# Grouped projection with keys and values first, roots kept per column, and rotation by copied halves

## The reference

```
def apply_rope(x, cos, sin):            # differential and grouped queries and keys
    x0, x1 = even and odd columns of a head
    out = stack([x0 * cos - x1 * sin, x0 * sin + x1 * cos])

q, k = rms_norm(q, gain), rms_norm(k, gain)   # per head of 64 columns
q, k = apply_rope(q), apply_rope(k)           # tokens only, not the context
attend(q, k, v)
```

## Time and profile before

| | |
|---|---|
| median of three runs | 2760.64 us |
| the profiled execution | 2751.36 us, span 2749.5 us |
| TensorE busy | 2554.8 us (93%) |
| VectorE busy | 1546.8 us (56%) |
| ScalarE busy | 901.0 us (33%) |
| GpSimd busy | 835.8 us (30%) |
| mean granted clock of TensorE | 0.955 of 2.4 GHz |
| chain that ended last | TensorE 77%, VectorE 12%, issue 5% of the span |

### The profile page before, as it was taken

One profiled execution on the slowest core, in us unless ns is written; L12 is line 12 of the kernel. 1 busy time (PEld: TensorE's weight loads), 2 busy tenths in 40 slices (PEclk: granted clock), 3 DMA queues, 4 the chain that ended last, 5 costly groups with the idle time before them and its releaser, 6 DMA issues.

```text
span 2749.5 us, 37446 instructions
## 1 busy us (share of the span) xinstructions
PE 2554.8 (93%) x14518; PEld 2085.7 (76%) x14518; DVE 1546.8 (56%) x2130; ACT 901.0 (33%) x1358; POOL 835.8 (30%) x445
## 2 busy tenths in 40 slices
PE   7899898999999988988989999999987997999998
PEld 5667886788877766866778888888775765788887
DVE  2366756667586765586455745645855475533232
ACT  3465123222233244345332122122224421433232
POOL 3333022554441221223222323222212320344443
PEclk9999998999998989999999999999987998999999
DMA  4212012545450100130023423322211020233222
GB/s 164 77 60 72 2 39 100 169 165 171 145 172 28 46 24 15 54 79 1 31 85 100 146 92 99 118 97 99 100 39 44 24 85 1 84 107 100 99 94 83
DMA packets 78422, 227.50 MB, mean 83 GB/s; under 512 B 21440, under 2 KB 23488, under 8 KB 77770
## 3 DMA queue, kind: packets, MB, share of 16 engines
q1 hardware_dynamic: 64056, 172.99, 19.2%
q10 hardware_dynamic: 14226, 52.54, 5.7%
HBM read 223.38 MB, written 2.12 MB: 82 GB/s over the span
## 4 chain that ended last, share of the span: by engine, by line
PE 77%; DVE 12%; issue 5%; ACT 2%; POOL 2%; DMA 0%; DVEq 0%; ACTq 0%; POOLq 0%
PE ps L270 19%; PE ps L271 19%; PE ps L272 19%; PE ps L732 3%; PE ps L747 3%; DVE rstd L641 2%; PE ps L763 2%; POOL w_lo L2183 2%; PE ps L410 1%; PE ps L341 1%; PE ps L343 1%; PE ps L342 1%; DVE ada_place L1004 1%; PE ps L2014 1%; PE ps L759 1%
## 5 line engine op out<-in xcount | busy, mean ns | idle before, releaser
L2183 POOL TENSOR_TENSOR w_lo<-ring,w_hi 128x1024 fp32r<-128x1024 f32 x293 | 714.4, 2438 | 1490.2 <-ACT w_hi L263 978.0
L270 PE MATMUL ps<-act_hi,w_hi 128*128 128x512 f32 x2264 | 841.6, 372 | 32.1 <-DVE mix_lo L915 10.9
L272 PE MATMUL ps<-act_hi,w_lo 128*128 128x512 f32 x2264 | 825.7, 365 | 0.0
L270 PEld LDWEIGHTS ps<-act_hi,w_hi 128*128 128x128 f32 x2264 | 428.3, 189 | 120.3 <-issue 21.0
L271 PE MATMUL ps<-act_lo_ffn,w_hi 128*128 128x512 f32 (+1 forms) x1408 | 514.4, 365 | 0.0
L272 PEld LDWEIGHTS ps<-act_hi,w_lo 128*128 128x128 f32 x2264 | 427.1, 189 | 72.3
L263 ACT CAST w_hi<-ring 128x1024 fp32r<-128x1024 f32 (+1 forms) x167 | 174.1, 1043 | 789.7 <-PE ps L272 671.8
L1004 DVE SCALAR_TENSOR_TENSOR ada_place<-ada_place 128x1024 f32<-128x1024 f32 x192 | 328.7, 1712 | 30.1 <-ACT ada_place L994 14.7
L271 PEld LDWEIGHTS ps<-act_lo_ffn,w_hi 128*128 128x128 f32 x1408 | 266.4, 189 | 42.2 <-issue 0.7
L1074 ACT CAST w_hi<-ring 128x1024 fp32r<-128x1024 f32 (+1 forms) x132 | 137.6, 1043 | 459.7 <-PE ps L272 459.7
L270 PE MATMUL ps<-hidden_hi,w_hi 128*128 128x512 f32 x704 | 256.7, 365 | 2.8 <-DVE hidden_lo L1140 1.6
(11 more groups left out here) (341 smaller groups left out, 3400.8 us busy)
## 6 DMA issues: line engine op xcount, KB each, us to landing
ring<-in_w_ffn SPq DMA_DIRECT2D x204, 512.0 KB, 3.3
ada_place<-in_w_ada ACTq DMA_DIRECT2D x96, 512.0 KB, 3.3
ring<-in_w_gdn SPq DMA_DIRECT2D x16, 512.0 KB, 3.3
ring<-in_w_hy SPq DMA_DIRECT2D x12, 512.0 KB, 3.3
ring<-in_w_dil_qk SPq DMA_DIRECT2D x8, 512.0 KB, 6.7
ring<-in_w_out SPq DMA_DIRECT2D x8, 512.0 KB, 3.3
ring<-in_w_diff_qk SPq DMA_DIRECT2D x8, 512.0 KB, 4.1
ring<-in_w_na_qk SPq DMA_DIRECT2D x8, 512.0 KB, 3.3
```

Source lines behind the costliest of these rows:

```text
L270: pe.matmul(out, w[0], x[0], start=start, stop=False)
L272: return pe.matmul(out, w[1], x[0], start=False, stop=stop)
L2183: pool.tensor_tensor(k.w_lo[:, a % SPLITS, :], k.ring[:, a % SLOTS, :], k.w_hi[:, a % SPLITS, :].bitcast(F32), ALU.subtract).then_inc(k.lo ...
```

## The change

There are three parts.

Rotation by halves. The columns of each head of the differential and grouped queries and keys are put in another order on the host: even ones in the first half of the head, odd ones in the second. The partner of a row is then 32 partitions away. ScalarE copies the tile from PSUM a second time, in four pieces of 32 partitions, each to the place of its partner (`swap_halves`), into one of two buffers in `mix`. VectorE multiplies the tile by gain and cosine, the swapped tile by the partner's gain and the signed sine, and adds (`rope_vector`). The rotation no longer needs the root, and the tile is multiplied by the reciprocal afterwards. The product with `rope_swap` goes.

Grouped projection. The order of units becomes keys, values, four of queries. Keys and values are the two units of `first_units`. Values are made like keys, copied to SBUF and turned by six transposes. For the queries the sums of squares are laid out with the tokens on the partitions and 8 columns (4 blocks x 2 heads), so root and reciprocal have 8 columns, not 512; eight products with the identity spread them again over the tile (`spread_roots`).

Feed-forward nets. ScalarE copies the upper halves of units 2 and 3 ahead of `ada_begin`.

```diff
-    ("w_gqa_qk", 5), ("w_gqa_v", 1), ("w_hy", 12), ("w_out_o", 8), ("w_ffn3", FFN_UNITS),
+    ("w_gqa", 6), ("w_hy", 12), ("w_out_o", 8), ("w_ffn3", FFN_UNITS),
...
+def swap_halves(s, dst, src):
+    for a in range(0, P, HD):
+        for to, at in ((a, a + HD // 2), (a + HD // 2, a)):
+            s.eng.copy(dst[to:to + HD // 2], src[at:at + HD // 2])
+def swapped(k, i):
+    return k.mix_flat[:, S * (i % 2):S * (i % 2 + 1)]
+def rope_vector(k, v, x, xs, gain, gain_swap):
+    link(v, v.eng.scalar_tensor_tensor(x, x, gain, k.const("cos", 0, S), ALU.mult, ALU.mult))
+    link(v, v.eng.scalar_tensor_tensor(xs, xs, gain_swap, k.const("sin", 0, S), ALU.mult, ALU.mult))
+    link(v, v.eng.tensor_tensor(x, x, xs, ALU.add))
...
-                else:
-                    pe.wait_ge(self.normed, self.b + j + 1)
-                    if j >= 1:
-                        pe.wait_ge(self.rotated, self.r + j)
-                    pe.matmul(k.bank(bank), k.const("rope_swap"), x[:, 0:S], start=True, stop=True).then_inc(self.swapped, 1)
...
             if i < n:
+                if self.jobs[i][5] is not None:
+                    if i >= 2:
+                        s.eng.wait_ge(self.normed, self.b + i - 1)
+                    swap_halves(s, swapped(k, i), src[:, 0:S])
                 s.eng.copy(back(x), blocks(src)).then_inc(self.evac, 1)
...
-                if what == "norm":
-                    v.eng.wait_ge(self.rooted, self.b + j + 1)
-                    if j < n:
-                        v.eng.wait_ge(self.evac, j + 1)
-                    link(v, v.eng.reciprocal(k.rstd[:, 0:size], k.probs[:, j % 2, 0:size]))
-                    v.eng.scalar_tensor_tensor(x, x, gain, k.rstd[:, 0:size], ALU.mult, ALU.mult).then_inc(self.normed, 1)
-                    v.eng.wait_ge(self.normed, self.b + j + 1)
+                if gain_swap is not None:
+                    v.eng.wait_ge(self.evac, self.e + j + 1)
+                    rope_vector(k, v, x[:, 0:S], swapped(k, j), gain, gain_swap)
+                v.eng.wait_ge(self.rooted, self.b + j + 1)
+                if j < n:
+                    v.eng.wait_ge(self.evac, self.e + j + 1)
+                link(v, v.eng.reciprocal(k.rstd[:, 0:size], k.probs[:, j % 2, 0:size]))
+                if gain_swap is None:
+                    ins = v.eng.scalar_tensor_tensor(x, x, gain, k.rstd[:, 0:size], ALU.mult, ALU.mult)
                 else:
-                    v.eng.wait_ge(self.swapped, self.r + j + 1)
-                    link(v, v.eng.tensor_tensor(k.probs_t[:, 0:S], k.bank(bank), k.const("sin", 0, S), ALU.mult))
-                    link(v, v.eng.tensor_tensor(x[:, 0:S], x[:, 0:S], k.const("cos", 0, S), ALU.mult))
-                    v.eng.tensor_tensor(x[:, 0:S], x[:, 0:S], k.probs_t[:, 0:S], ALU.add).then_inc(self.rotated, 1)
-                    v.eng.wait_ge(self.rotated, self.r + j + 1)
+                    v.eng.tensor_tensor(x[:, 0:S], x[:, 0:S], k.rstd[:, 0:S], ALU.mult)
+                    ins = v.eng.scalar_tensor_tensor(x[:, S:size], x[:, S:size], gain, k.rstd[:, S:size], ALU.mult, ALU.mult)
+                ins.then_inc(self.normed, 1)
+                v.eng.wait_ge(self.normed, self.b + j + 1)
...
-                upper(it, 2 * a, static and c == 0 and a == 0)
+                begun = static and c == 0 and a == 0
+                if not begun:
+                    upper(it, 2 * a)
...
-                upper(it, 2 * a + 1)
+                if not begun:
+                    upper(it, 2 * a + 1)
...
         if c == 0:
+            upper(0, 0, True)
+            upper(0, 1)
             f.ada_begin(s)
...
+def gqa_bank(t):
+    return 4 if t % 2 == 0 else 0
+def gqa_project_tensor(k, pe):
+    v0, evac = FIRST["w_gqa"], k.sem("gqa_evac")
+    squares, summed, rooted, normed = k.sem("head_squares"), k.sem("head_summed"), k.sem("head_rooted"), k.sem("head_normed")
+    first_units(k, pe, "w_gqa", k.h_hi, k.lo2, (S, CTX), (k.sem("norm_lo"), DT * LOWERED.index("mod_a1")))
+    def add(t):
+        job = GQA + 1 + t
+        pe.wait_ge(squares, job + 1)
+        pe.wait_ge(rooted, job)
+        for b in range(PAIRS):
+            last = pe.matmul(k.bank(6, 2, 2 * b), k.sq[:, (t + 1) % 2, b * P:(b + 1) * P], k.const("heads64")[:, 0:P:HD],
+                             start=True, stop=True)
+        last.then_inc(summed, 1)
+    def spread_roots(t):
+        pe.wait_ge(k.sem("gqa_inverted"), t + 1)
+        if t >= 1:
+            pe.wait_ge(normed, GQA + 1 + t)
+        for b in range(PAIRS):
+            for h in range(2):
+                at, r = 32 + 8 * (t % 2) + 2 * b + h, slice(HD * h, HD * h + HD)
+                last = pe.matmul(k.ps[r, 7 * 512 + b * P:7 * 512 + (b + 1) * P], k.small[:, at:at + 1].broadcast_to([P, HD]),
+                                 k.const("ident"), start=True, stop=True)
+        last.then_inc(k.sem("gqa_spread"), 1)
+    for t in range(4):
+        u = v0 + SPLITS + t
+        if t >= 1:
+            pe.wait_ge(evac, (1, 3, 4)[t - 1])
+        if u not in HALVED:
+            pe.wait_ge(k.lo_done, u + 1)
+        unit_products(k, pe, gqa_bank(t) // 2, u, k.h_hi, k.lo2, DT, (S,))
+        if t == 0:
+            pe.wait_ge(squares, GQA + 1)
+            pe.matmul(k.bank(6), k.const("heads64"), k.sq[:, 0, 0:S], start=True, stop=True)
+            pe.matmul(k.bank(7, CTX), k.const("heads64"), k.sq[:, 0, S:T], start=True, stop=True).then_inc(summed, 1)
+            pe.wait_ge(evac, 2)
+            for b in range(6):
+                last = pe.transpose(k.bank(5, P, b * P) if b < 4 else k.bank(1, P, (b - 4) * P),
+                                    k.probs[:, 1, b * P:(b + 1) * P], k.const("ident"))
+            last.then_inc(k.sem("gqa_turned"), 1)
+        else:
+            add(t - 1)
+        if t >= 2:
+            spread_roots(t - 2)
+    add(3)
+    spread_roots(2)
+    spread_roots(3)
+def gqa_project_scalar(k, s):
     q, key, val = gqa_views(k)
-    return Projection(k, "w_gqa_qk", 5, "w_gqa_v", 1, P, val, 28, 8, turned=0, jobs=
-                      [(q[:, t, 0:S], k.const("heads64"), k.par("gqa_q"), "eps_query", float(HD), True) for t in range(4)]
-                      + [(key[:, 0, :], k.const("heads64"), k.par("gqa_k"), "eps", 1.0, True)])
+    u0, evac = FIRST["w_gqa"], k.sem("gqa_evac")
+    squares, summed, rooted, normed = k.sem("head_squares"), k.sem("head_summed"), k.sem("head_rooted"), k.sem("head_normed")
+    s.eng.wait_ge(k.unit_done, u0 + 1)
+    split_ahead(k, s, u0 + 1 + SPLITS)
+    s.eng.activation(k.sq[:, 0, 0:T], k.ps[:, 0:T], ACT.Square).then_inc(squares, 1)
+    swap_halves(s, swapped(k, 0), k.bank(0))
+    s.eng.copy(key[:, 0, :], k.ps[:, 0:T]).then_inc(evac, 1)
+    split_ahead(k, s, u0 + 2 + SPLITS)
+    s.eng.copy(k.probs[:, 1, 0:T], k.ps[:, 1024:1024 + T]).then_inc(evac, 1)
+    def root(t):
+        s.eng.wait_ge(summed, GQA + 2 + t)
+        s.eng.activation(k.small[:, 16 + 8 * (t % 2):24 + 8 * (t % 2)], k.bank(6, 8), ACT.Sqrt, bias=k.par("eps_query"),
+                         scale=float(HD)).then_inc(rooted, 1)
+    for t in range(4):
+        s.eng.wait_ge(k.unit_done, u0 + SPLITS + t + 1)
+        split_ahead(k, s, u0 + 2 * SPLITS + t + 1)
+        src = k.bank(gqa_bank(t))
+        if t >= 1:
+            s.eng.wait_ge(summed, GQA + t)
+        s.eng.activation(k.sq[:, (t + 1) % 2, 0:S], src, ACT.Square).then_inc(squares, 1)
+        if t >= 1:
+            s.eng.wait_ge(normed, GQA + t)
+        swap_halves(s, swapped(k, t + 1), src)
+        s.eng.copy(q[:, t, 0:S], src).then_inc(evac, 1)
+        if t == 0:
+            s.eng.wait_ge(summed, GQA + 1)
+            s.eng.activation(k.probs[:, 0, 0:T], k.ps[:, 6 * 512:6 * 512 + T], ACT.Sqrt, bias=k.par("eps"))\
+                .then_inc(rooted, 1)
+        else:
+            root(t - 1)
+        if t == 1:
+            s.eng.wait_ge(k.sem("gqa_turned"), 1)
+            link(s, s.eng.copy(val[:, 0:4, :], k.bank(5).rearrange("p (b n) -> p b n", b=4)))
+            link(s, s.eng.copy(val[:, 4:6, :], k.bank(1, CTX).rearrange("p (b n) -> p b n", b=2)))
+    root(3)
+def gqa_project_vector(k, v):
+    q, key, _ = gqa_views(k)
+    evac, rooted, normed = k.sem("gqa_evac"), k.sem("head_rooted"), k.sem("head_normed")
+    v.eng.wait_ge(evac, 1)
+    rope_vector(k, v, key[:, 0, 0:S], swapped(k, 0), k.par("gqa_k"), k.par("gqa_k_swap"))
+    v.eng.wait_ge(rooted, GQA + 1)
+    link(v, v.eng.reciprocal(k.rstd[:, 0:T], k.probs[:, 0, 0:T]))
+    v.eng.tensor_tensor(key[:, 0, 0:S], key[:, 0, 0:S], k.rstd[:, 0:S], ALU.mult)
+    v.eng.scalar_tensor_tensor(key[:, 0, S:T], key[:, 0, S:T], k.par("gqa_k"), k.rstd[:, S:T], ALU.mult, ALU.mult)\
+        .then_inc(normed, 1)
+    for t in range(4):
+        v.eng.wait_ge(evac, 3 + t)
+        rope_vector(k, v, q[:, t, 0:S], swapped(k, t + 1), k.par("gqa_q"), k.par("gqa_q_swap"))
+        v.eng.wait_ge(rooted, GQA + 2 + t)
```

(8 more changed lines are left out.)

116 lines of the change are left out of this document (51 added, 65 removed).

## The result

The changed kernel took 2717.53 us, median of four runs (2712.32 to 2719.03), against 2759.5 us (2757.52 to 2763.11) for the kernel before: ratio 0.9843, 95% interval 0.9825 to 0.9861. The forecast was 2720, in a range of 2707 to 2733. The profiled execution took 2716.32 us, its span is 2714.5 us; before these were 2751.36 and 2749.5. So the two profiles differ by 35.0 us and the medians by 42: the profiled execution of before lay 8 to 9 us under its kernel's median, that of after 1.2.

The account below looks back on a forecast made before the run. TensorE was taken to bound the kernel, by its stands and low-clock stretches. Terms 31.4 + 3.4 + 0 + 4.6 + 1.2 = 40.6 us took the profiled 2751.36 to 2710.8; the 9.3 offset gave 2720 us, range 2707 to 2733.

Parts of the forecast that it names:

- Grouped projection, 31.4: Grouped projection: without narrow value products and with 8-column roots, the attention starts at 2055.6 instead of 2087.0, gaining 31.4 us.
- the spread: Grouped projection's tail: sixteen narrow fp32 products that spread the query roots over the tile were to take 4.0 us.
- The rival "Clock": Grouped unit 3 at clock 0.50 throughout and differential values at low clock longer: 5.5 + 2 us lost, 2728; chance 0.15.
- Swap copy, 0.52: ScalarE, both projections: one crosswise copy of 32 partitions x 512 from PSUM costs 0.52 us, bounds 0.37 and 1.03.
- copies dear: Rival, both projections: crosswise copies cost so much that the kernel is slower, 2772 us at 1.6 each; chance 0.03.
- Differential projection, 3.4: Differential projection: shorter tile period, earlier value product and two rotating products fewer gain 3.4 us (−1 to +6).
- The loop: Differential projection: swaps, copy and root on ScalarE, then VectorE's reciprocal and products, with two buffers, set 10.05 us a tile.
- the value product, which needs that, starts 2.0 earlier: Differential projection: with tile 7 swapped and copied at 940.5, the value product starts 2.0 us before 942.55.
- VectorE shut out: Rival, differential projection: each rotation meets a whole GpSimd subtraction, 1.0 us a tile lost over six tiles, 2726; chance 0.04.
- First net, 0: First feed-forward net's start: the wait moves to unit 4, which starts at 475.9; gain 0 us (−2.5 to +2).
- Second net, 4.6: Second feed-forward net's start: unit 4 starts earlier, 7.7 less 3.1 for a slower restart, gain 4.6 us (2 to 6.5).
- Third net, 1.2: Third feed-forward net's start, without conditioning: TensorE's wait and its restart go, gain 1.2 us.

Follow-up runs that it names:

- a_onecopy: The changed kernel with one straight copy in place of the four crosswise ones, leaving the rotation out in effect: 2692.77 us, ratio 0.9764.
- b_ffn: The kernel before with only the reordered start of the feed-forward nets on ScalarE: 2757.31 us, ratio 1.0004.
- a_noffn: The changed kernel with the old start of the feed-forward nets: 2720.03 us, ratio 0.9862.
- b_pad: The kernel before with four unused columns in the parameters, as many as the change adds: 2758.06 us, ratio 1.0008.
- a_dmafirst: The changed kernel with the conditioning's DMAs issued first, then the splits of units 2 and 3, then Silu: 2709.1 us, ratio 0.9834.
- a_turn: The changed kernel with the old rotation in the differential projection: 2716.96 us, ratio 0.9848.

## Why the prediction came out, point by point

*The total* is right partly by luck. The terms summed to 40.6, the profiles differ by 35.0; and I carried the offset of 9.3 between the profile of before and its median over to a profile of after that lay 1.2 from its median. The two errors, 5.6 too much gain and 8 too much offset, cancel. How large the first is, one pair of profiles cannot say: the second profile of the changed kernel is 40.2 us below that of before, and the medians differ by 42 and, measured again, by 44.8.

*Grouped projection, 31.4: mechanism right, 3 us too small.* 34.5 in the first pair of profiles, 34 to 38 over all pairs. The size that was off is the spread: sixteen spreading products take 1.97, not 4.0, and two such spreads lie in the tail, which is 4.1 shorter than counted; unit 3 ended 1.0 later. My row has products that write 128 rows, these write 64; that this is the reason is not shown. The rival "Clock" fell: unit 3 began at the lower level but left it 2.6 us into the unit. The stage ran at a mean clock of 0.75 before and 0.87 after. Of the edits inside the stage only the column roots were taken out alone, 2 to 4 us; how the rest divides between the order of the units, the values made like keys and the new rotation no run shows.

*Swap copy, 0.52: 0.59.* Four took 2.35. The step stands; "copies dear" is refuted, and the price of the whole is shown by a_onecopy.

*Differential projection, 3.4: failed, 0.4 on the average of the profiles.* The loop was right: 10.16 for 10.05, broken by a third buffer. What failed is the line "the value product, which needs that, starts 2.0 earlier". Counted from the norm's spread it started at 93.8 in the four profiles with the old rotation and at 94.9 in the six with the new: 1.1 later. Of the 3.1 between, 0.6 are the first reciprocal (4.8 later where I had 4.2), 1.6 the first period of 11.66, in which a product met GpSimd's subtraction (2.19 for 0.69: the rival "VectorE shut out", once instead of six times), and 0.6 the five others at 0.11 each. Behind the value product 0.5 to 2 us came back, as forecast for the two rotating products and the longer stand.

*First net, 0: its own step right, the stage wrong.* Unit 4 started at 475.81, less 0.7 for the later start of the stage 475.1, for 475.9; b_ffn gives 0.65 of gain, a_noffn 0.9. The 4 us lost belong to the rhythm, which a_noffn and b_pad show without this edit. No step of the forecast had looked at the down units.

*Second net, 4.6: 4.0 in this profile, but not a fixed size.* In seven profiles of the edit it is between 1.2 and 4.1 against a_noffn, and 0 in b_ffn: the term goes with the landing of four late DMAs (see b_ffn). I had set the delay of the issue and not the landing. a_dmafirst, which takes the delay away, gives the 4 to 6 on top.

*Third net, 1.2: 1.4.*

*Clock, beyond what was forecast.* The new rotation's stage ran at a mean of 0.94 to 0.96 in the six profiles with two buffers, with the old one at 0.96 to 0.98 in four; windows over the stage, a_turn, then the changed kernel's second run:

```profile
855.90:990.20 134.30, 127.78 (x594) 100.79 (x594) 97.47 (x76) 41.42 (x56) 28.23 (x13) 0.97 0.13 44
```

```profile
854.80:988.30 133.50, 120.12 (x580) 97.39 (x582) 90.42 (x83) 60.33 (x88) 29.00 (x13) 0.95 0.13 44
```

TensorE has 7.7 us less to do there and the stage is 0.8 shorter; the longer stands come with more time at 1.2 GHz. I cannot say from these how much of the 7 the clock cost by itself.

## What to carry to other kernels

When an engine's work is replaced by another's, write down the loop through both queues and count its buffers: a third buffer of 512 columns brought more (5 us here, 4 in the grouped projection) than the new rotation did. In an in-order queue, ask of each new instruction who stands behind it: the root behind the copies, and the DMA issue behind the splits, cost more than the instruction itself. And before a term is read off one pair of profiles, look whether the stages beside it moved: here an untouched loop tipped from 4.6 to 5.3 us a unit on a tie of 10 ns, as large as most terms of the sum.

## What the runs showed of the hardware

- Four crosswise copies of 32 partitions x 512 columns from PSUM take 2.35 us, 0.59 from start to start, a little more than copies of 128 partitions (four in 2.06, 0.48 from start to start): a quarter of the partitions costs no less.
- VectorE's product with two operands in SBUF and GpSimd's subtraction exclude each other; a reciprocal did not: in the changed kernel the one at 898.28 took its 4.95 us beside a subtraction at 900.53 that took its 2.40. When both ask within 10 ns, the record's earlier start does not say who wins: GpSimd's was 0.01 us the earlier both times, and lost once.
- Two engines that take turns like this can lock into one of two stable rhythms, 4.61 and 5.31 us, for the rest of a loop.
